# Two-block transformer on one core: quadrant turns by transposes, rotary halves swapped off TensorE

## The reference, cut to what matters

```
# gated delta rule, chunks of 64, both directions, 16 heads
a = where(strict, (kb @ k^T) * decay, 0)
t_inv = triangular_solve(eye + a, eye)          # 64x64 unit triangular inverses

# attention layer: heads of 128 = row half and column half of 64, each rotated
x1, x2 = split(x, 2)                            # 32 and 32
rope = concat([x1 * cos - x2 * sin, x2 * cos + x1 * sin])

# MLA: 8 query heads of 64 + 32; the last 32 are rotated the same way (16 and 16),
# and one rotated 32-wide key part is shared by all heads
```

## Time and profile before, and how to read it

| | |
|---|---|
| median of 3 runs | 2802.83 us (2799.78 to 2813.41) |
| the profiled execution, its own time | 2801.93 us |
| span of its profile | 2800.1 us |
| PE busy | 2665.0 us |
| PE weight loads | 1822.2 us |
| DVE, ACT, POOL busy | 1493.9, 934.2, 373.2 us |
| mean granted PE clock | 0.986 of 2.4 GHz |

### The profile page before, as it was taken

How to read it: one execution, slowest core, us unless ns; L and a number is a source line. 1 busy time by engine, 2 the same in 40 slices (tenths; PEclk the granted TensorE clock), 3 DMA queues, 4 the chain that set the end, 5 groups by cost and what they waited for, 6 DMA issues and landing times.

```text
span 2800.1 us, 36489 instructions
## 1 busy us (share of the span) xinstructions
PE 2665.0 (95%) x14724; PEld 1822.2 (65%) x14724; DVE 1493.9 (53%) x2932; ACT 934.2 (33%) x2233; POOL 373.2 (13%) x276
## 2 busy tenths in 40 slices
PE   7899999999999999999999889999999999999997
PEld 3567767667676576646544337677767663788886
DVE  4387786787876636422332435433365322777722
ACT  1436456465463530032343223222224312211200
POOL 0221121220211000000000121232022120000031
PEclk9999999999999999999999999999999999999999
DMA  5221321312213426020001011112221212122220
GB/s 234 72 46 44 92 59 45 77 31 82 59 44 97 128 89 232 39 98 30 30 31 38 26 70 52 61 61 91 109 102 46 90 47 104 61 91 91 83 83 30
DMA packets 108328, 209.30 MB, mean 75 GB/s; under 512 B 82272, under 2 KB 88224, under 8 KB 96640
## 3 DMA queue, kind: packets, MB, share of 16 engines
q1 hardware_dynamic: 85728, 202.48, 21.0%
q10 hardware_dynamic: 22432, 4.49, 0.9%
HBM read 195.32 MB, written 11.63 MB: 74 GB/s over the span
## 4 chain that ended last, share of the span: by engine, by line
PE 82%; DVE 8%; ACT 6%; DMA 2%; issue 1%; SPq 1%; ACTq 0%; DVEq 0%
PE ps L1876 10%; PE ps L1424 10%; PE ps L2080 9%; PE ps L1331 8%; PE ps L1625 6%; PE ps L2108 5%; PE ps L1893 3%; PE ps L2020 3%; PE ps L1754 2%; PE ps L1506 2%; PE ps L1491 2%; PE ps L1766 2%; ACT arena L2138 1%; PE ps L1740 1%; DVE arena L2912 1%
## 5 line engine op out<-in xcount | busy, mean ns | idle before, releaser
L2137 ACT ACTIVATE arena<-ps 128x256 f32<-128x256 f32 (+10 forms) x703 | 274.4, 408 | 773.8 <-PE ps L1876 157.8
L1424 PE MATMUL ps<-arena 128*128 128x385 f32 x1232 | 425.4, 494 | 16.0 <-ACT arena L2137 14.9
L1424 PEld LDWEIGHTS ps<-arena 128*128 128x128 f32 x1232 | 227.8, 191 | 163.9 <-POOL arena L3510 13.8
L1876 PE MATMUL ps<-arena 128*128 128x256 f32 x1456 | 327.7, 379 | 2.0 <-ACT arena L2137 2.0
L1876 PEld LDWEIGHTS ps<-arena 128*128 128x128 f32 x1456 | 270.4, 190 | 40.5 <-issue 5.7
L2080 PE MATMUL ps<-arena 128*128 128x256 f32 x1176 | 254.6, 378 | 0.0
L2080 PEld LDWEIGHTS ps<-arena 128*128 128x128 f32 x1176 | 222.1, 189 | 32.8 <-issue 0.5
L1331 PE MATMUL ps<-arena 128*128 128x512 f32 x496 | 220.2, 602 | 14.8 <-DVE arena L3175 5.1
L1331 PEld LDWEIGHTS ps<-arena 128*128 128x128 f32 x496 | 94.6, 192 | 138.8 <-issue 127.5
L2138 ACT ACTIVATE arena<-ps,arena 128x128 f32<-128x128 f32 x544 | 157.1, 378 | 46.4 <-PE ps L1559 25.5
L1625 PE MATMUL ps<-arena 128*128 128x512 f32 (+1 forms) x512 | 172.0, 491 | 0.3 <-DVE arena L3004 0.3
(11 more groups left out here) (363 smaller groups left out, 4183.1 us busy)
## 6 DMA issues: line engine op xcount, KB each, us to landing
arena<-in_ada_w SPq DMA_DIRECT2D x12, 2048.0 KB, 8.9
arena<-in_w_up SPq DMA_DIRECT2D x11, 2048.0 KB, 7.7
arena<-in_w_dil SPq DMA_DIRECT2D x9, 2048.0 KB, 7.7
arena<-in_w_dn SPq DMA_DIRECT2D x8, 2048.0 KB, 10.5
arena<-gsum SPq DMA_DIRECT2D x24, 512.0 KB, 5.4
arena<-in_w_gate SPq DMA_DIRECT2D x6, 2048.0 KB, 7.6
arena<-in_w_down SPq DMA_DIRECT2D x4, 2816.0 KB, 9.5
arena<-in_att_in SPq DMA_DIRECT2D x5, 2048.0 KB, 7.5
```

The source lines that it names most:

```text
L1424: m = e.matmul(ps[:, bank, 0:HALF_PAD], left[:, k], right[:, k], start=first and k == 0, stop=k == 3, skip_group_check=not first)
L1876: m = e.matmul(ps[:, bank, 0:256], left[:, k], right[:, k], start=first and k == 0, stop=k == 3, skip_group_check=not first)
L2137: return e.activation(out, x, ACT.Copy)
```

## The change

In `join_x` and `halves_x` the quadrant 0:64 is turned by `e.transpose`, the quadrant 64:128 still by a product. In the attention layer the permutation is gone: VectorE multiplies each group of 32 partitions with signed sines and writes the result to the partitions of its partner, in four operations. In the MLA the swap of the two 16-partition halves is made by two transfers inside SBUF for the key part and two for each pair of heads, issued by ScalarE's queue, and VectorE rotates two heads in one operation; a pair's transfers wait until the pair two before is rotated, since they use the same place. The two permutation tables leave the constants (224 of their columns).

```diff
@@ axial_tables
-    return np.concatenate([np.cos(ang), np.sin(ang)], 1).astype(np.float32)
+    sign = np.where(np.arange(128) % 64 < 32, np.float32(1), np.float32(-1))[:, None]
+    return np.concatenate([np.cos(ang), sign * np.sin(ang)], 1).astype(np.float32)
@@ program
+        swapped = [arena[:, a:a + 1024] for a in (top[0], WORDS - 4096 - 1024)]
@@ join_x (halves_x likewise, with 2 * h + d and h)
-                        m = e.matmul(un64(ps[U, b, :], u), quadrant(Yf, 2 * g, u, U, U), turner(U), start=True, stop=True)
+                        x, o = quadrant(Yf, 2 * g, u, U, U), un64(ps[U, b, :], u)
+                        if U.start:
+                            m = e.matmul(o, x, turner(U), start=True, stop=True)
+                        else:
+                            e.transpose(o, x, turner(U))
@@ tensor_program, heads_norm
-                if 0 <= t - 1 < 10:
-                    r = t - 1
-                    x = qT4[:, r * 512:(r + 1) * 512] if r < 8 else kT2[:, (r - 8) * T_ALL + 256:(r - 7) * T_ALL]
-                    e.wait_ge(*at("qkn_x", r))
-                    take_banks(6)
-                    e.matmul(ps[:, 6, :], K("perm"), x, start=True, stop=True).then_inc(*mark("qk_rot", r))
-                    leave_banks(("qk_sin", r), 6)
@@ tensor_program, MLA
-            e.wait_ge(*at("kr_ev"))
-            take_banks(5)
-            e.matmul(ps[0:96, 5, :], perm96, kr[0:96], start=True, stop=True).then_inc(*mark("kr_rot"))
-            leave_banks(("kr_x", 0), 5)
...
-                e.wait_ge(*at("uq_ev", h))
-                take_banks(5 + h % 2)
-                e.matmul(ps[0:96, 5 + h % 2, :], perm96, qm[0:96, h * 512:(h + 1) * 512], start=True, stop=True).then_inc(
-                    *mark("uq_rot", h))
-                leave_banks(("uq_x", h, 0), 5 + h % 2)
...
-                        e.wait_ge(*at("uq_x", h, 2))
+                        e.wait_ge(*at("uq_x", h // 2, 2))
@@ scalar_program
+            def swap(x, to, *name):
+                e.dma_start(to[64:80], x[80:96]).then_inc(*landed(name[0] + "0", *name[1:]))
+                e.dma_start(to[80:96], x[64:80]).then_inc(*landed(name[0] + "1", *name[1:]))
+
+            e.wait_ge(*at("kr_ev"))
+            swap(kr, swapped[1][:, 0:512], "kr_swap")
             for h in range(8):
                 e.wait_ge(*at("uq_pe", h))
                 copy(qm[0:96, h * 512:(h + 1) * 512], ps[0:96, h % 4, :]).then_inc(*mark("uq_ev", h))
+                if h % 2:
+                    p = h // 2
+                    e.wait_ge(*at("uq_ev", h))
+                    if p:
+                        e.wait_ge(*(at("uq_x", p - 2, 2) if p > 1 else at("kr_x", 2)))
+                    swap(qm[:, p * 1024:(p + 1) * 1024], swapped[p % 2], f"uq_swap{p % 2}_", p)
...
-            e.wait_ge(*at("uq_x", 7, 2))
+            e.wait_ge(*at("uq_x", 3, 2))
@@ vector_program, rotate
-                e.wait_ge(*at("qk_rot", t))
+                e.wait_ge(*at("qkn_x", t))
                 e.wait_ge(*at("in_ax"))
                 if t:
                     e.wait_ge(*at("qk_x", t - 1))
-                e.tensor_tensor(sqb1[:, 0:512], ps[:, 6, :], ax[:, 512:1024], MUL).then_inc(*mark("qk_sin", t))
+                for a in (0, 32, 64, 96):
+                    m = e.tensor_tensor(sqb1[a ^ 32:(a ^ 32) + 32, 0:512], x[a:a + 32], ax[a:a + 32, 512:1024], MUL)
+                m.then_inc(*mark("qk_sin", t))
+                e.wait_ge(*at("qk_sin", t))
                 e.tensor_tensor(x, x, ax[:, 0:512], MUL).then_inc(*mark("qk_cos", t))
@@ vector_program, rotate96
+            def rotate96(x, other, name, *which):
+                n = x.shape[1] // 512
+                x, other = (y[ROT].rearrange("p (h n) -> p h n", h=n) for y in (x, other))
+                e.tensor_tensor(other, other, bc(sinT[ROT], 1, [32, n, 512]), MUL).then_inc(*mark(name, *which, 0))
+                e.tensor_tensor(x, x, bc(cosT[ROT], 1, [32, n, 512]), MUL).then_inc(*mark(name, *which, 1))
+                e.wait_ge(*at(name, *which, 0))
+                e.wait_ge(*at(name, *which, 1))
+                e.tensor_tensor(x, x, other, ADD).then_inc(*mark(name, *which, 2))
+
+            e.wait_ge(*at("sin"))
+            e.tensor_scalar(sinT[64:80], sinT[64:80], -1.0, None, MUL).then_inc(*mark("sin_minus"))
...
+            for i in range(2):
+                e.wait_ge(*at(f"kr_swap{i}"))
+            rotate96(kr, swapped[1][:, 0:512], "kr_x")
+            for p in range(4):
+                for i in range(2):
+                    e.wait_ge(*at(f"uq_swap{p % 2}_{i}", p))
+                rotate96(qm[:, p * 1024:(p + 1) * 1024], swapped[p % 2], "uq_x", p)
```

More of the change, by code:

```diff
@@ L153 @@
 for _name, _w in [("ident", 128), ("ones", 128), ("tri", 256), ("strict", 256), ("join", 128),
-                  ("perm", 128), ("perm96", 96), ("eps", 1), ("lnq", 1), ("invf", 1)]:
+                  ("eps", 1), ("lnq", 1), ("invf", 1)]:
     CONST[_name] = (NCONST, NCONST + _w)
@@ L172, in constants @@
     put("join", np.concatenate([r % 64 // b == 2 * (x // b) + 1 - d for b in (16, 32) for d in range(2)], 1))
[L173 to L184, removed]
     put("eps", EPS)
@@ L959, in program @@
         SCAN = list(zip([0, 1, 2, 3, 4, 5], [1, 0, 5, 4, 3, 2]))
-        perm96 = cst[0:96, CONST["perm96"][0]:CONST["perm96"][1]]
         P96 = slice(0, 96)
@@ L1518, in halves_x @@
                         U = UPPER[d]
-                        m = e.matmul(un64(ps[U, b, :], h), quadrant(Yf, 2 * g, 2 * h + d, U, U), turner(U),
-                                     start=True, stop=True)
+                        x, o = quadrant(Yf, 2 * g, 2 * h + d, U, U), un64(ps[U, b, :], h)
+                        if U.start:
+                            m = e.matmul(o, x, turner(U), start=True, stop=True)
+                        else:
+                            e.transpose(o, x, turner(U))
                 m.then_inc(*mark("inv_pe", j, g, "x", 64))
@@ L3088, in rotate @@
                     e.wait_ge(*at("qk_x", t - 1))
-                e.tensor_tensor(sqb1[:, 0:512], ps[:, 6, :], ax[:, 512:1024], MUL).then_inc(*mark("qk_sin", t))
+                for a in (0, 32, 64, 96):
+                    m = e.tensor_tensor(sqb1[a ^ 32:(a ^ 32) + 32, 0:512], x[a:a + 32], ax[a:a + 32, 512:1024], MUL)
+                m.then_inc(*mark("qk_sin", t))
+                e.wait_ge(*at("qk_sin", t))
                 e.tensor_tensor(x, x, ax[:, 0:512], MUL).then_inc(*mark("qk_cos", t))
-                e.wait_ge(*at("qk_sin", t))
                 e.wait_ge(*at("qk_cos", t))
@@ L3212, in vector_program @@
             ROT = slice(64, 96)
-            def rotate96(x, b, name, *which):
-                e.tensor_tensor(sqb2[ROT], ps[ROT, b, :], sinT[ROT], MUL).then_inc(*mark(name, *which, 0))
-                e.tensor_tensor(x[ROT], x[ROT], cosT[ROT], MUL).then_inc(*mark(name, *which, 1))
+            def rotate96(x, other, name, *which):
[4 more added lines that the diff above has]
+                e.wait_ge(*at(name, *which, 0))
                 e.wait_ge(*at(name, *which, 1))
-                e.tensor_tensor(x[ROT], x[ROT], sqb2[ROT], ADD).then_inc(*mark(name, *which, 2))
+                e.tensor_tensor(x, x, other, ADD).then_inc(*mark(name, *which, 2))
+            e.wait_ge(*at("sin"))
+            e.tensor_scalar(sinT[64:80], sinT[64:80], -1.0, None, MUL).then_inc(*mark("sin_minus"))
             e.wait_ge(*at("cos"))
-            e.wait_ge(*at("kr_rot"))
-            rotate96(kr, 5, "kr_x")
-            for h in range(8):
-                e.wait_ge(*at("uq_rot", h))
-                e.wait_ge(*(at("uq_x", h - 1, 2) if h else at("kr_x", 2)))
-                rotate96(qm[:, h * 512:(h + 1) * 512], 5 + h % 2, "uq_x", h)
+            e.wait_ge(*at("sin_minus"))
+            for i in range(2):
[5 more added lines that the diff above has]
+                rotate96(qm[:, p * 1024:(p + 1) * 1024], swapped[p % 2], "uq_x", p)
             def seven_adds(tag, i, p, name):
```

## The result

| | before | after |
|---|---|---|
| median of the runs taken together | 2805.36 us (4 runs) | 2930.61 us (4 runs, 2923.91 to 2935.2) |
| the profiled execution, its own time | 2801.93 us | 2935.2 us |
| its span | 2800.1 us | 2933.4 us |
| mean granted PE clock | 0.986 | 0.958 |

What follows compares the result with a forecast made beforehand. PE was taken as the bound, busy 95% of a 2800.1 us span. Sum: 2801.9 - 8.6 (attention) - 16.1 (MLA) + 100.8 (joins) = 2878 us; 8-in-10 range 2790 to 2965.

Steps and rivals of the forecast that it cites:

- Form change: Join batches: each transpose/product pair changes the array's form twice, taking 0.475 us instead of 0.117, +100.8 us in all.
- The price of a block: Join batches: 0.15 us that every block of quadrant instructions pays whatever its length.
- The clock: Join batches: likeliest case had the clock hold, as today's full-clock batches don't lower it and PE never stops for long.
- case A: Join batches: form changes are paid, without a fall of the clock; 2878 us, chance 0.42.
- B: Join batches: the clock falls to 1.2 GHz on top of the form changes, 68 us more, 2946; chance 0.36.
- Rival C: Join batches: no change of form, transpose runs side by side with the upper product; PE loses 24.7 us, 2777; chance 0.14.
- D: Join batches: side by side is lost but nothing is drained; +16.8 us, 2794; chance 0.08.
- Attention: Attention rotation: ten permutation products leave PE at 0.86 us each, 8.6 us saved; VectorE's longer step stays hidden.
- MLA: MLA rope: nine products and their waits leave PE, 1.8 us at the kr block and 14.3 over eight heads, 16.1 saved.
- twice as long still fits: MLA rope: swap transfers taken as 4.1 us to landing; even doubled, they would be ready before PE needs them.

Runs made afterwards that it cites:

- experiment 2: The whole change, but each group's lower quadrants are all transposed first and its upper ones multiplied after (grouped order); 2814.93 us, ratio 1.0038 to before.
- the wide products: The whole change, but the joins' lower quadrants are turned by products 128 columns wide instead of transposes, alternating with 64x64 upper products; 3031.24 us, ratio 1.0804 to before.
- joins only: The kernel before with only join_x and halves_x as in the change, both rotations as before; 2953.23 us, ratio 1.0526.
- rope only: The kernel before with only MLA's rope as in the change, constants and addresses as before; 2789.93 us, ratio 0.9947.
- experiment 7: Each rotation's change alone in the kernel before: attention's 2796.93 us, ratio 0.9973; MLA rope's 2789.93 us, ratio 0.9947.
- experiment 8: Both rotations as in the change, joins of before, and SyncE holds the 2 MB load until the last swap has landed; 2785.65 us, ratio 0.9931 to before.
- rotations only: The change with the joins of the kernel before, so only both rotations are changed; 2789.70 us, ratio 0.9945 to before.

## Why the prediction was right in its sign and low in its size

*Form change.* Right in kind: a 64x64 transpose among 64x64 products is another form, each pair changes twice, and experiment 2 shows that this and not the transpose is paid. The term was oversized: 0.475 us for a pair, 0.43 measured, 87.8 us for all in place of 100.8. The price of a block that I had read from whole batches, 0.15, is 0.128 between blocks this short.

*The clock.* This is the step that failed. I gave case A 0.42 and B 0.36 and so forecast 2878 instead of B's 2946; the result lies between them and nearer to B. The argument was "none of today's batches at full clock brings it down, and PE never stops for long in the new ones". Today's batches alternate two quadrants side by side and are no measure for batches that stand still most of the time, and a stop long enough to be seen as idle isn't needed: the windows above are 100% busy. The other half of my own paragraph, that the array stands still for most of a pair, was the better guide. B's terms were close: I put 68 us on the clock, the account gives 65, of which 5.8 are longer waits. That it came so close is in part luck, since two errors offset each other: there are 150 us more of low clock where I had 136, and each costs 0.43 or less where I had 0.50. The split was off too: 10.2 to 17.1 us behind most long batches where I had 13.6, 30.7 for the first, 3.4 to 6.8 for each short one where I had 3.4.

The Trainium skill (TensorE: Matmul & The Clock Gate, Part 4) says that transposes don't count as activity for the clock as products do. Here that isn't what decides, by the rows: the grouped run has as many transposes and is at 1.2 GHz for 51 us of the delta layer, before for 41, while the wide products, with none in the joins, are at 287. What in these batches brings the clock down isn't shown beyond this: the time at 1.2 GHz grows with the density of form changes, and is longer still where the same pairs are spread out (246 us) or a change takes longer (287).

*Rival C and D.* Refuted by the batch alone: 10.3 us at full clock, against 2.9 and 4.2.

*Attention.* 8.6 us predicted, 8.6 in its stage, by the step of 7.73 and the hidden VectorE work. *MLA.* 16.1 predicted, 16.1 in its stage. But in after 6.5 us more pass from its first score to the end: 1.5 of wait, and low stretches that before doesn't have at 1805.3 (3.4 us) and that are longer at 2348.0 (6.8 instead of 3.4), at 2498.2 and 2511.9 (10.2 instead of 3.4). The long late ones are in joins only too, without the change of the rope, and are absent from rope only (experiment 7), so only the wait and the stretch at 1805.3 go with the rope: some 1.7 to 2.4 us. What fell short is the last link of the rope's step, "twice as long still fits": it measured the swap against PE's arrival at the first score. It left out that the freed 2 MB load starts just before the last swap (I had it only as coming "16 us earlier with everything else"), and that the softmax stands behind the rotation in VectorE's queue.

*The sum of the stages:* 2801.9 - 1.0 + 87.8 + 65.2 - 8.6 - 10.2 = 2935.1, but for rounding the profiled execution's own 2935.2. It closes by construction, since the 65.2 is a difference; what tests it is the last column of the account.

## What to carry to other kernels

Order PE's instructions by form: a change between fp32 transposes and quadrant products costs 0.128 us here, about as much as two passes of 0.058, so a saved pass is worth nothing if it alternates. A row that says "busy" doesn't say "streaming": when an edit fills PE's queue with short instructions and standstill, count the time that the clock is low as well, and charge it a little under half (0.40 to 0.45 here). Distributing such work over the timeline made it worse here (246 us low instead of 191); gathering the instructions of one form healed it (51). Work taken off PE by way of a transfer is paid in the queue that waits for the transfer; look at what the freed buffer starts at that moment, and hold it back if it has slack (here that made the swap land in time; a gain in the kernel's time isn't shown).

## What I had not expected of the hardware

- The clock goes to 1.2 GHz inside a batch without any idle time in PE's rows, and the time at 1.2 GHz grows with the density of form changes: 10, 24, 75 and 150 us more of it for groups of eight, four, two and one.
- A pair at 1.2 GHz takes 0.64 us, not 0.86: of a form change's 0.128 us little depends on the clock (an estimate: if a pass takes twice its 0.058 us, some 0.145 is left for each change).
- A transfer of 16 partitions of 1024 elements inside SBUF lands 2.3 us after its issue by the median of eight in experiment 8; the last pair's two, with a 2 MB load under way, take 7.0 and 7.9 in rotations only. The Trainium skill (SBUF — State Buffer, The DMA setup-cost knee) fits a transfer by 2 us and its bytes at 436 GB/s, an estimate of 2.15 for 64 KB; the quiet transfers are near that, the ones beside the load aren't.
- A 32x1024 operation on two SBUF operands takes VectorE 1.22 us alone and 2.1 to 2.3 beside GpSimd's 128x512 sums, and GpSimd's sum 1.27 alone and 2.15 then. The one that starts first isn't slowed (VectorE's of 1796.81, 1.22 us, in the rows of the result), and each next one ends 1.1 us after the one that it overlaps (1798.03, 1799.16, 1800.24): they read as taking turns, not as sharing. The Trainium skill (GPSIMD Engine Reference, Specifications) names this contention for VectorE instructions with two SBUF inputs; the trace agrees.
